# Attention sinks as an extra probability column, and mLSTM memory products placed on strips and row groups, in a two-layer decoder step

## The chip, the core and the metric

The kernel runs on one core of a Trainium2 chip. TensorE (PE) multiplies matrices out of SBUF into PSUM, VectorE (DVE) and ScalarE (ACT) do elementwise work, GpSimd (POOL) and SyncE (SP) issue DMAs. Each engine runs its own instruction stream in order, and streams meet at semaphores. The metric is the device time of one execution in microseconds, the lower the better.

## The reference, cut to what matters

Layer 0 is sliding-window attention with a learned sink per head, layer 1 an mLSTM (a matrix memory). There are 512 prompt tokens and 8 sequences with 4 sample tokens each.

```python
# layer 0, per head: the sink takes part in the maximum and in the sum, not in the output
s = einsum(q, k) * HEAD_DIM ** -0.5 + bias            # 128 queries x 256 keys per block
mx = maximum(max(s), sink)
p = exp(s - mx)
p = p / (sum(p) + exp(sink - mx))
o = p @ v

# layer 1, per head (8 of them), sample tokens: each sequence b has its own memory S[b], 128 x 256
num = a * (qs @ S) + qk @ v
S_new = a_last * S + einsum('s,sd,se->de', wts, k, v)
```

Around them each layer has an input projection, a gate, an output projection and norms over 2048 channels.

## The kernel before

**Weight products.** All large products go through `block`: a weight block of 128 output channels is split into a high and a low part (`w_hi` by ACT in `round_hi`, `w_lo` by DVE in `split_lo`), and for each of 16 tiles of the contraction PE does six matmuls of 272 columns (line 750) into a pair of PSUM banks (`PJ`). A block is called an entry. `PHASES` gives the entries of each phase: `l0` has 8 entries in each of three turns of a loop, `l0z` 10, `l1` 8 for each of 8 heads ("QKVVZOZO").

**Points.** The small work of attention and of the memory is inserted between tiles of the product. In layer 0 every entry has four points, after tiles 4, 8, 11 and 15 (`POINTS`), numbered p = 4e + i (`attend_points`). In the mLSTM every entry has two, after tiles 7 and 15 (`memory_points`): points 0 to 7 of a head lie in its last four entries, point 8 in the first entry of the next head. ACT and DVE have functions `attend(m, p)` and `memory(m, p)` of the same names. In each entry they first empty `PJ` of the entry before, then split the next weights, then do the points; what stands first in this order is done first.

**Attention, per group m (4 of them).** There are 16 softmax steps x; a step is 128 queries of one head in two query blocks, 2 x 256 scores. `scores` makes two steps in one go (line 867), into `MX` banks 0 and 1. `soft` on DVE adds the bias (line 1643), takes the maximum (1645), compares it with the negated sink (1647), and forms the exponent of the sink (1648). ACT does exp of both halves (1242) and of the sink (1244). `norm` on DVE adds the sink's term (1653), takes the reciprocal (1654) and scales (1657). `p_turn` on PE transposes the probabilities (876), ACT copies them out (1235), `pv` multiplies with the values (890), `gate_prompt` on DVE multiplies into the gate (1667). Step x has its `soft` at point 10 + x, its `norm` at 11 + x, its `p_turn` at 12 + x, so at every point from 10 to 28 something is done.

**mLSTM memory, per head.** At point 0 PE transposes k and v (1004, and 1006 for the 32 sample tokens); at 1 it makes k q and spreads three rows of gates over all partitions with weights of 8 rows (1014, 1017); at 2 it makes the chunk updates (1026 to 1031); at 4 the prompt's output (1040 to 1046); at 5 the sample's output; at 7 the update of the eight sample memories `cs` (1065), which DVE adds in (1941); at 8 the norm sums (1072, 1075). Of point 5 the inner part is, for each half of the channels and each of the 8 sequences, one matmul of a 128x128 piece of memory with 4 columns:

```python
mm(MX[:, 3, TS * blk:TS * blk + TS], vs[:, P * blk:P * blk + P], Ds[0:TS, :], start=True, stop=False)   # 1052
for b in range(NB):                                                                                     # 1055
    mm(MX[:, 3, TS * blk + ND * b:TS * blk + ND * b + ND], cs[:, b, P * blk:P * blk + P],
       qa[:, TP + ND * b:TP + ND * b + ND], start=False, stop=(b == NB - 1))
```

An f32 matmul shows as two records in the trace, each with a weight load of its own; an instruction list names it once.

Of the kernel before, what the change touches and what calls it, by code (L numbers as in the profile page):

```python
# [29 lines left out]
P = 128  # L30
# [25 lines left out]
ATT_POINTS = 29  # L56
# [32 lines left out]
C_FIX = 305  # L89
C_NEGD, C_NEGS = 305, 305 + 768  # L90
C_L0 = C_NEGS + 1056
C_CM, C_SM, C_BM = C_L0, C_L0 + 128, C_L0 + 160
C_ALL = C_L0 + 168

def constants():
# [31 lines left out]
    c[0:TS, C_BM:C_BM + NB] = (np.arange(TS)[:, None] // ND == np.arange(NB)[None, :])  # L128
# [7 lines left out]
def offsets(sizes, at=0):  # L136
    out = {}
    for name, size in sizes:
# [10 lines left out]
              ("soft", 1536), ("negd", 768), ("negs", 1056)])  # L149
A1 = offsets([("q", T), ("k", T), ("v", 2 * T), ("vtok", 4 * DV), ("wk", 4 * P), ("rows", 3 * T),  # L150
              ("S", 4 * DV), ("n", 8), ("D", TP), ("qa", T), ("qn", T), ("emt", T), ("h", 2 * T),
              ("cs", NB * DV), ("sb", 3 * TS), ("Ds", TS), ("Uc", 40), ("wc", 40), ("wb", 64),
              ("nsT", 64), ("nout", 72), ("cm", 128), ("sm", 32), ("bm", 8)])
# [36 lines left out]
def trunk(nc, x_prompt, x_sample, c_prompt, c_sample, cache_k, cache_v, state_C, state_n, state_m,  # L190
# [3 lines left out]
    with ExitStack() as ctx:  # L194
# [53 lines left out]
        PP = [soft[:, 0:512], soft[:, 512:1024]]  # L248
        PT = [soft[:, 1024:1536], misc[:, 0:TP]]
# [6 lines left out]
        rows = area(A1, "rows")  # L256
        wks = rows[0:TS, 0:1024].rearrange("p (b e) -> p b e", b=NB)
        ksv = rows[0:TS, 1024:1408]
        ks, vs = ksv[:, 0:P], ksv[:, P:3 * P]
        wbh = rows[0:TS, 1408:1416]  # L260
        GP = slice(64, 64 + MH)
        BP = slice(96, 96 + MH)
        R = rows[GP, :].rearrange("p (j t) -> p j t", j=3)
        RB = rows[BP, :].rearrange("p (j t) -> p j t", j=3)
# [10 lines left out]
        wb = area(A1, "wb").rearrange("p (h b) -> p h b", h=MH)  # L275
        nsT = area(A1, "nsT").rearrange("p (b h) -> p b h", b=NB)
# [62 lines left out]
        om_done, zg_done = sem("om_done"), sem("zg_done")  # L339

# [11 lines left out]
        hout_done, hsq_done = sem("hout_done"), sem("hsq_done")  # L352
        cu_ready, cnew_done, ss1_ready = sem("cu_ready"), sem("cnew_done"), sem("ss1_ready")
# [209 lines left out]
        def _(pool):  # L563
# [92 lines left out]
            pool.dma_start(bm, const[:, C_BM:C_BM + 8]).then_inc(gl_in, 16)  # L656
# [7 lines left out]
            pool.dma_start(nm_p.rearrange("o b h -> h (o b)"), R[:, 2, TP - 1:TP], **SLOW).then_inc(Sp_out, 16)  # L664
            pool.dma_start(nm_s[0].rearrange("b h -> h b"), R[:, 2, TP:T].rearrange("p (b t) -> p b t", t=ND)[:, :, 3], **SLOW)\
# [40 lines left out]
        def _(pe):  # L706
# [164 lines left out]
            def p_turn(m, x):  # L871
# [3 lines left out]
                for c in range(4):  # L875
                    last = tr(MX[:, 2, P * c:P * c + P], PP[x % 2][:, P * c:P * c + P], ident)  # L876
# [19 lines left out]
            def attend(m, p):  # L896
# [1137 lines left out]
```

## Time and profile before

| | |
|---|---|
| median of 3 runs | 2447.22 us (2441.83 to 2449.89) |
| the profiled execution | 2441.93 us, its span 2440.3 us |
| granted TensorE clock over the span | 0.952 |
| PE busy | 2282.1 us, 94% of the span |
| weight product, line 750 | 13152 matmuls in three groups, 293 to 300 ns each |
| one turn of the layer 0 loop | 141.8 us |
| DMA | 300.68 MB, 123 GB/s in the mean |

Durations of matmuls overlap with their neighbours, so a stretch is measured from the start of one row to the start of the next. The number in brackets behind a row of a timeline is the time that its engine stood idle before it, and who ended that. A granted clock of 1.00 is full speed, 0.50 half.

### The profile page before, as it was taken

Reading aid. Unit: us, or ns where it says so; the run is one execution under the profiler, and the core shown is the slowest. Engines: PE = TensorE matmul, PEld = TensorE weight load, DVE = VectorE, ACT = ScalarE, POOL = GpSimd, SP = SyncE. Lnnn points to the kernel's source line nnn. Section 1 sums busy time; section 2 is a strip of 40 time slices with the busy share of each in tenths; the row PEclk is TensorE's granted clock in tenths of the full one; section 3 lists DMA queues with packets and bytes.
Section 4 is the critical chain, followed back from the end, with each engine's and each line's share of the span. In section 5 each row is a group of like instructions: output and inputs, shape, how many; then the busy total and the mean of one; then the engine's idle time right before and its main releaser. Section 6 shows DMA issues by size and latency. Waiting matters only on the chain.

```text
span 2440.3 us, 41297 instructions
## 1 busy us (share of the span) xinstructions
PE 2282.1 (94%) x17089; PEld 2075.9 (85%) x17089; DVE 989.2 (41%) x1561; ACT 682.1 (28%) x1113; POOL 65.2 (3%) x108
## 2 busy tenths in 40 slices
PE   5879999999989999987999999999999999989996
PEld 2469888898988977776999998999999889988995
DVE  1152555737456412137533424343434334352225
ACT  1232343424334322124312212221212121222222
POOL 1000000000000000000000000000000000000000
PEclk8889999999999999988999998999999899989998
DMA  8953213122211599942428346534255345419622
GB/s 319 388 192 87 79 53 90 53 74 69 73 53 53 161 300 297 295 143 98 106 65 100 61 100 75 104 63 107 70 98 70 83 76 96 80 52 294 210 70 74
DMA packets 345755, 300.68 MB, mean 123 GB/s; under 512 B 8561, under 2 KB 287337, under 8 KB 344473
## 3 DMA queue, kind: packets, MB, share of 16 engines
q1 hardware_dynamic: 335952, 247.87, 40.8%
q0 software_dynamic: 9360, 50.19, 5.8%
q8 instruction: 134, 2.20, 0.4%
q10 hardware_dynamic: 290, 0.27, 0.0%
q14 instruction: 19, 0.16, 0.0%
HBM read 274.81 MB, written 27.56 MB: 124 GB/s over the span
## 4 chain that ended last, share of the span: by engine, by line
PE 77%; DVE 8%; DMA 7%; issue 4%; ACT 2%; DVEq 1%; ACTq 0%; SPq 0%
PE PJ L750 59%; DMA obuf<-in_w_ada 3%; DMA raw<-in_w_in_mlstm 3%; PE MX L938 3%; PE MX L1055 1%; ACT w_hi L1148 1%; PE MX L1065 1%; PE MX L876 1%; PE MX L1017 1%; PE MX L867 1%; DVE arena L1643 1%; DVE st L1645 1%; PE MX L890 1%; DMA raw<-in_w_in_attn 1%; DVE w_lo L1497 1%
## 5 line engine op out<-in xcount | busy, mean ns | idle before, releaser
L750 PE MATMUL PJ<-h_hi,w_hi 128*128 128x272 f32 x4384 | 955.1, 300 | 50.9 <-DVE h_lo L1555 23.8
L750 PE MATMUL PJ<-h_hi,w_lo 128*128 128x272 f32 x4384 | 925.0, 293 | 0.0
L750 PE MATMUL PJ<-h_lo,w_hi 128*128 128x272 f32 x4384 | 923.8, 293 | 0.1
L750 PEld LDWEIGHTS PJ<-h_hi,w_hi 128*128 128x128 f32 x4384 | 707.7, 194 | 128.2 <-issue 106.1
L750 PEld LDWEIGHTS PJ<-h_lo,w_hi 128*128 128x128 f32 x4384 | 708.9, 194 | 0.3 <-issue 0.3
L750 PEld LDWEIGHTS PJ<-h_hi,w_lo 128*128 128x128 f32 x4384 | 704.1, 194 | 0.0
L1497 DVE TENSOR_TENSOR w_lo<-raw,w_hi 128x2048 fp32r<-128x2048 f32 x106 | 242.9, 2292 | 431.5 <-ACT w_hi L1148 431.5
L1148 ACT ACTIVATE w_hi<-raw 128x2048 fp32r<-128x2048 f32 x106 | 202.0, 1906 | 42.9 <-DMA raw<-in_w_in_mlstm 33.1
L1242 ACT ACTIVATE arena<-arena,st 128x256 f32<-128x256 f32 x128 | 64.1, 501 | 145.4 <-DVE st L1648 145.4
L1423 ACT ACTIVATE arena<-PJ 128x544 f32<-128x544 f32 x32 | 20.0, 625 | 247.1 <-PE PJ L750 247.1
L1771 DVE COPY modT<-MX 128x36 f32 x16 | 3.1, 196 | 210.6 <-PE MX L949 210.6
L1749 DVE TENSOR_TENSOR w_lo<-raw,w_hi 128x2048 fp32r<-128x2048 f32 x30 | 68.7, 2291 | 36.3 <-ACT w_hi L1324 36.3
L1643 DVE SCALAR_TENSOR_TENSOR arena<-arena,fix,MX 128x512 f32<-128x512 f32 x64 | 47.7, 745 | 68.3 <-PE MX L867 36.6
L1756 DVE TENSOR_TENSOR arena<-arena 128x544 f32<-128x544 f32 x32 | 23.2, 725 | 118.6 <-ACT arena L1315 116.4
L1315 ACT ACTIVATE arena<-PJ 128x544 f32<-128x544 f32 x32 | 20.0, 625 | 177.2 <-PE PJ L750 170.6
L938 PE MATMUL MX<-arena,cT 128*32 128x512 f32 x512 | 68.2, 605 | 0.0
L716 PE MATMUL PJ<-obuf,cT 128*32 128x512 f32 x256 | 42.3, 754 | 26.7 <-DMA obuf<-in_w_ada 26.6
L876 PE MATMUL MX<-fix,arena 128*128 128x128 f32 x256 | 42.1, 288 | 24.4 <-DVE arena L1657 24.4
L1337 ACT ACTIVATE misc<-MX 105x512 f32<-105x512 f32 x16 | 9.6, 598 | 195.2 <-PE MX L938 195.2
L876 PEld LDWEIGHTS MX<-fix,arena 128*128 128x128 f32 x256 | 27.3, 141 | 40.2 <-issue 27.6
L1972 DVE SCALAR_TENSOR_TENSOR obuf<-misc,obuf 128x544 f32 (+1 forms) x16 | 11.6, 725 | 122.7 <-ACT misc L1415 122.7
L1324 ACT ACTIVATE w_hi<-raw 128x2048 fp32r<-128x2048 f32 x30 | 57.5, 1918 | 0.0
(301 smaller groups left out, 1907.2 us busy)
## 6 DMA issues: line engine op xcount, KB each, us to landing
arena<-in_w_ada SPq DMA_DIRECT2D x64, 1024.0 KB, 5.2
raw<-in_w_in_mlstm SPq DMA_DIRECT2D x64, 1024.0 KB, 14.7
raw<-in_w_in_attn SPq DMA_DIRECT2D x40, 1024.0 KB, 5.7
obuf<-in_w_ada SPq DMA_DIRECT2D x32, 1024.0 KB, 10.0
raw<-in_w_out_attn SPq DMA_DIRECT2D x16, 1024.0 KB, 7.9
raw<-in_w_out_mlstm SPq DMA_DIRECT2D x16, 1024.0 KB, 5.9
x_spill<-arena POOLq DMA_DIRECT2D x2, 4352.0 KB, 12.5
arena<-x_spill POOLq DMA_DIRECT2D x2, 4352.0 KB, 14.0
```

Source lines behind the costliest of these rows:

```text
L716: last = mm(PJ[32 * j:32 * j + 32, 2 * pair, :], c_cols(4 * q + j), obuf[:, 4 * (u % 4) + j, 0:512], start=(q == 0), stop=(q == 3))
L750: last = mm(PJ[:, 2 * pair + f, 0:HT], w, h[:, k, HT * f:HT * f + HT], start=(k == 0 and n == 0), stop=(k == KT - 1 and n == 2))
L867: last = mm(MX[:, half, 256 * bl:256 * bl + 256], q0[hs, j, P * b:P * b + P], kk[hs, P * b:P * b + 2 * P], start=True, stop=True)
L876: last = tr(MX[:, 2, P * c:P * c + P], PP[x % 2][:, P * c:P * c + P], ident)
L890: last = mm(MX[64 * half:64 * half + 64, 3, P * bl:P * bl + P], vtok[:, P * (b - 1 + kb) + 64 * a:P * (b - 1 + kb) + 64 * a + 64], PT[half ...
L938: last = mm(MX[32 * i:32 * i + 32, 2, :], c_cols(4 * j + i), u_raw[j][:, 512 * i:512 * i + 512], start=(j == 0), stop=(j == STRIPS - 1))
L1148: fn(w_hi[s][:, :], raw[s][:, :], ACT.Copy).then_inc(hi_done, 1)
L1242: fn(pb, pb, ACT.Exp, bias=st[:, o + 2 + bl:o + 3 + bl], accum_out=st[:, o + 6 + bl:o + 7 + bl]).then_inc(pexp_ready, 1)
L1324: fn(w_hi[s][:, :], raw[s][:, :], ACT.Copy).then_inc(hi_done, 1)
L1497: tt(w_lo[s][:, :], raw[s][:, :], w_hi[s][:, :].bitcast(F32), ALU.subtract)\
L1643: chain(stt(pb, negd[:, 256 * bp:256 * bp + 512], fix[:, ds(head + C_SLP, 1)], MX[:, half, :], ALU.mult, ALU.add))
L1749: tt(w_lo[s][:, :], raw[s][:, :], w_hi[s][:, :].bitcast(F32), ALU.subtract).then_inc(lo_done, 1)
```

## The change

**Attention.** The probability rows get a 257th column for each of the two query blocks, so `PP` is 2 x 257 wide. ACT writes the sink there before the softmax. The maximum and the exp with its running sum then run over 257 columns and take in the sink; lines 1647, 1648, 1244 and 1653 go. A pair of steps is handled at each even point: `p_turn`, `scores`, `p_turn` on PE, two `soft` and two `norm` on DVE, copies and exps on ACT. `pv` and `gate_prompt` go to the odd points. There are 28 points instead of 29.

**mLSTM.** The three gate rows `R` lie on partitions 0, 32 and 64, so the three matmuls of point 1 use three row groups of PE and three banks. Sample k and v are written four times, once to each strip of 32 partitions (point 0, 12 matmuls instead of 3 transposes). At point 5 the queries are the weights, 32 columns, in four column strips, and the memories move, 256 columns; each strip gets the product of all 32 queries with one sequence's memory. ACT copies this out, and a new point 6 picks the right rows with a constant (`C_SS`) and adds them to the rest. At point 7 the eight updates use four row groups and four banks.

```diff
@@ PE attend @@
-                if 14 <= p < ATT_POINTS and p % 2 == 0:
-                    pv(m, (p - 14) // 2)
+                if p >= 12 and p % 2 == 0:
+                    p_turn(m, p - 12)
                 if 10 <= p < 26 and p % 2 == 0:
                     scores(m, (p - 10) // 2)
-                if 0 <= p - 12 < 16:
-                    p_turn(m, p - 12)
+                if p >= 12 and p % 2 == 0:
+                    p_turn(m, p - 11)
+                if p >= 13 and p % 2:
+                    pv(m, (p - 13) // 2)
@@ ACT attend @@
-                    fn(st[:, o + 8:o + 10], st[:, o + 4:o + 6], ACT.Exp).then_inc(pexp_ready, 1)
+                        if x + 2 < 16:
+                            head = g * 8 + (2 * ((x + 2) // 4) + x % 2)
+                            fn(PP[x % 2][:, :, 2 * P:PB], nsink[:, ds(head, 1)].unsqueeze(1).broadcast_to([P, 2, 1]),
+                               ACT.Copy, scale=-1.0).then_inc(sink_set, 1)
@@ DVE soft and norm @@
-                chain(tt(st[:, o + 2:o + 4], st[:, o:o + 2], nsk, ALU.min))
-                tt(st[:, o + 4:o + 6], st[:, o + 2:o + 4], nsk, ALU.subtract).then_inc(pmax_ready, 1)
+                dve.wait_ge(sink_set, val(0, 16, m, x + 1))
+                dve.tensor_reduce(st[:, o:o + 2], pb, AX, ALU.max, negate=True).then_inc(pmax_ready, 1)
-                chain(tt(st[:, o + 10:o + 12], st[:, o + 6:o + 8], st[:, o + 8:o + 10], ALU.add))
@@ PE memory, points 0, 1, 5 and 6, 7 @@
-                        last = tr(MX[0:TS, 3, P * j:P * j + P], src[:, TP:T], ident)
+                        for i in range(4):
+                            last = mm(MX[32 * i:32 * i + 32, 3, P * j:P * j + P], src[:, TP:T], ident,
+                                      start=True, stop=True)
-                        last = mm(MX[:, 1 + j, :], fix[BP, C_ONE:C_ONE + P], RB[:, j, 0:TP],
+                        last = mm(MX[:, 1 + j, :], fix[32 * j:32 * j + MH, C_ONE:C_ONE + P], RB[j],
                                   start=True, stop=True)
+                    pe.wait_ge(abs_done, val(0, 1, m, 1))
+                    for b in range(NB):
+                        j, c = b % 4, b // 4
+                        last = mm(MX[32 * j:32 * j + 32, 2, DV * c:DV * c + DV], qa[:, TP:T], cs[:, b, :],
+                                  start=True, stop=True)
+                    last.then_inc(qc_ready, 1)
+                if p == 6:
+                    pe.wait_ge(qg_done, val(0, 1, m, 1))
                     for blk in range(2):
-                        mm(MX[:, 3, TS * blk:TS * blk + TS], vs[:, P * blk:P * blk + P], Ds[0:TS, :],
-                           start=True, stop=False)
-                        for b in range(NB):
-                            mm(MX[:, 3, TS * blk + ND * b:TS * blk + ND * b + ND],
-                               cs[:, b, P * blk:P * blk + P], qa[:, TP + ND * b:TP + ND * b + ND],
-                               start=False, stop=(b == NB - 1))
+                        o = MX[:, 3, TS * blk:TS * blk + TS]
+                        mm(o, vs[0:TS, P * blk:P * blk + P], Ds[0:TS, :], start=True, stop=False)
+                        for c in range(2):
+                            mm(o, Dm[:, DV * c + P * blk:DV * c + P * blk + P], fix[:, C_SS + TS * c:C_SS + TS * c + TS],
+                               start=False, stop=(c == 1))
-                        last = mm(MX[:, b // 2, DV * (b % 2):DV * (b % 2) + DV], wks[:, b, :], vs,
-                                  start=True, stop=True)
+                        j, c = b % 4, b // 4
+                        rows = slice(32 * j, 32 * j + TS)
+                        last = mm(MX[:, j, DV * c:DV * c + DV], wks[rows, c, :], vs[rows, :], start=True, stop=True)
@@ ACT memory, point 5 (the abs of the sample's sums and the squares go to point 6) @@
+                    act.wait_ge(qc_ready, val(0, 1, m, 1))
+                    act.wait_ge(hp_done, val(0, 1, m, 1))
+                    fn(Dm, MX[:, 2, :], ACT.Copy).then_inc(qg_done, 1)
@@ DVE memory, point 0 @@
-                    ts(rows[BP, :], rows[GP, :], fix[GP, ds(h + (C_ID + 64), 1)], None, ALU.mult).then_inc(rb_done, 1)
+                    ts(RBt[0:GP.stop, :], Rt[0:GP.stop, 0:TP], fix[0:GP.stop, ds(h + C_OH, 1)], None, ALU.mult).then_inc(rb_done, 1)
+                    tt(RS[0:GP.stop], Rt[0:GP.stop, TP:T].unsqueeze(1).broadcast_to([GP.stop, 3, TS]),
+                       O3[0:GP.stop, :, ds(h, 1)].broadcast_to([GP.stop, 3, TS]), ALU.mult).then_inc(rb_done, 1)
-                    tt(wks, MX[0:TS, 3, 0:P].unsqueeze(1).broadcast_to([TS, NB, P]),
+                    tt(wks, MX[:, 3, 0:P].unsqueeze(1).broadcast_to([P, 2, P]),
```

**In what order it stands.** DVE in an attention group, one softmax step and the next, before. Line 1643 is the bias, 1645 the maximum, 1653 to 1657 the normalisation; rows on registers are what the loop needs.

```order
L1643 SCALAR_TENSOR_TENSOR arena<-arena,fix,MX 128x512
L180 REGISTER_ALU
L1645 TENSOR_REDUCE st<-arena 128x2
L180 REGISTER_ALU
L1647 TENSOR_TENSOR st<-st,nsink 128x2
L180 REGISTER_ALU
L1648 TENSOR_TENSOR st<-st,nsink 128x2
L1652 REGISTER_ALU
L1653 TENSOR_TENSOR st<-st 128x2
```

The same place after; 1684 is the bias, 1688 the maximum, 1693 and 1696 the normalisation.

```order
L1684 SCALAR_TENSOR_TENSOR arena<-arena,fix,MX 128x2x256
L191 REGISTER_ALU
L1687 REGISTER_ALU
L1688 TENSOR_REDUCE st<-arena 128x2
L1684 SCALAR_TENSOR_TENSOR arena<-arena,fix,MX 128x2x256
L191 REGISTER_ALU
L1687 REGISTER_ALU
L1688 TENSOR_REDUCE st<-arena 128x2
L1692 REGISTER_ALU
L1693 RECIPROCAL st<-st 128x2
L191 REGISTER_ALU
L1696 TENSOR_SCALAR arena<-arena,st 128x256 x2
```

Two steps now stand in front of the first normalisation, and three of the small operations are gone.

PE at point 5 of an mLSTM head, before, between the weight product (750).

```order
L750 MATMUL PJ<-h_hi,w_lo 128x272 x2
L1052 MATMUL MX<-arena 128x32
L1055 MATMUL MX<-arena 128x4 x8
L1052 MATMUL MX<-arena 128x32
L1055 MATMUL MX<-arena 128x4 x8
L1058 MATMUL MX<-arena,fix 128x32
L1059 MATMUL MX<-arena,fix 128x32
L750 MATMUL PJ<-h_hi,w_hi 128x272 x2
```

After, point 5 (the product is line 765):

```order
L765 MATMUL PJ<-h_hi,w_lo 128x272 x2
L1075 MATMUL MX<-arena 32x256 x8
L765 MATMUL PJ<-h_hi,w_hi 128x272 x2
```

and half a block later point 6, where nothing stood:

```order
L765 MATMUL PJ<-h_hi,w_lo 128x272 x2
L1083 MATMUL MX<-arena 128x32
L1085 MATMUL MX<-fix,arena 128x32 x2
L1083 MATMUL MX<-arena 128x32
L1085 MATMUL MX<-fix,arena 128x32 x2
L1087 MATMUL MX<-arena,fix 128x32
L1088 MATMUL MX<-arena,fix 128x32
L765 MATMUL PJ<-h_hi,w_hi 128x272 x2
```

Sixteen matmuls of four columns became eight of 256 at one point and four of 32 at the next.

## Rows read from the trace of the kernel before

**Rows 1.** The page: engine busy times, and the chain's shares.

```profile
PE 2282.1 (94%) x17089; PEld 2075.9 (85%) x17089; DVE 989.2 (41%) x1561; ACT 682.1 (28%) x1113; POOL 65.2 (3%) x108
...
PE 77%; DVE 8%; DMA 7%; issue 4%; ACT 2%; DVEq 1%; ACTq 0%; SPq 0%
```

**Rows 2.** The page's groups: count | busy, mean ns | idle before, ended by.

```profile
L876 PE MATMUL MX<-fix,arena 128*128 128x128 f32 x256 | 42.1, 288 | 24.4 <-DVE arena L1657 24.4
```

**Rows 3.** Timeline of PE, attention: start, duration, line, form, count, idle before.

```profile
415.02 1.13 PE L867 MATMUL MX<-arena 64*128 64x256 f32 x8
416.08 0.65 PE L876 MATMUL MX<-fix,arena 128*128 128x128 f32 x4
...
421.15 0.65 PE L876 MATMUL MX<-fix,arena 128*128 128x128 f32 x4 [1.41 <-DVE arena L1657]
...
706.18 1.11 PE L876 MATMUL MX<-fix,arena 128*128 128x128 f32 x4 [4.08 <-DVE arena L1657]
```

**Rows 4.** Timelines of DVE and of ACT, one softmax step.

```profile
421.85 0.75 DVE L1643 SCALAR_TENSOR_TENSOR arena<-arena,fix,MX 128x512 f32<-128x512 f32 x1 [0.82 <-PE MX L876]
...
423.35 0.16 DVE L1647 TENSOR_TENSOR st<-st,nsink 128x2 f32<-128x2 f32 x1
...
424.04 0.61 DVE L1657 TENSOR_SCALAR arena<-arena,st 128x256 f32<-128x256 f32 x2
...
423.74 0.51 ACT L1242 ACTIVATE arena<-arena,st 128x256 f32<-128x256 f32 x1 [1.30 <-DVE st L1648]
...
424.74 0.19 ACT L1244 ACTIVATE st<-st 128x2 f32<-128x2 f32 x1
```

**Rows 5.** Timeline of PE, points 0 and 1 of head 1.

```profile
1330.85 0.49 PE L1006 MATMUL MX<-fix,arena 128*32 128x128 f32 x3
1331.10 0.49 PE L750 MATMUL PJ<-h_hi,w_hi 128*128 128x272 f32 x2
...
1338.17 2.84 PE L1017 MATMUL MX<-arena,fix 8*128 8x512 f32 x6
```

**Rows 6.** Timeline of PE, points 5 and 7 of head 2.

```profile
1508.23 0.41 PE L750 MATMUL PJ<-h_hi,w_lo 128*128 128x272 f32 x2
1508.57 0.40 PE L1052 MATMUL MX<-arena 32*128 32x32 f32 x2
1508.90 1.95 PE L1055 MATMUL MX<-arena 128*128 128x4 f32 x16
...
1513.57 0.50 PE L750 MATMUL PJ<-h_hi,w_hi 128*128 128x272 f32 x2
...
1527.30 3.72 PE L1065 MATMUL MX<-arena 32*128 32x256 f32 x16
```

**Rows 7.** Stretches: us, busy and counts, PEclk, DMA share, GB/s; sums of eight and seven.

```profile
342.28:483.99 141.71, 135.71 (x1140) 124.75 (x1139) 80.85 (x181) 57.13 (x137) 4.12 (x6) 1.00 0.25 69
...
706.95:711.31 4.36, 4.36 (x21) 4.11 (x19) 2.61 (x8) 1.78 (x6) 0.00 (x0) 0.50 0.15 37
...
1485.71:1497.83 12.12, 12.12 (x97) 12.12 (x97) 7.25 (x18) 3.12 (x5) 0.56 (x1) 1.00 0.61 52
...
1378.56:1393.30 14.74, 14.74 (x97) 14.60 (x97) 0.77 (x3) 1.40 (x3) 0.00 (x0) 0.81 0.27 60
...
sum 113.88, PE 113.88 PEld 112.71 DVE 6.15 ACT 11.21 POOL 0.00; mean PE 14.23 PEld 14.09 DVE 0.77 ACT 1.40 POOL 0.00
...
sum 55.24, PE 55.24 PEld 54.21 DVE 29.52 ACT 0.32 POOL 6.67; mean PE 7.89 PEld 7.74 DVE 4.22 ACT 0.05 POOL 0.95
...
1852.63:1861.45 8.82, 8.82 (x50) 8.82 (x50) 4.11 (x4) 2.37 (x6) 0.00 (x0) 0.66 0.60 107
```

**Rows 8.** Timeline of PE: 64-column strips in attention, 32-column strips in out0.

```profile
384.08 1.15 PE L848 MATMUL MX<-arena 128*64 128x64 f32 x16
...
857.05 1.07 PE L938 MATMUL MX<-arena,cT 128*32 128x512 f32 x8
```

**Rows 9.** Waits of ACT in the mLSTM: total, times, longest.

```profile
ACT w_hi L1148 <- DMA raw<-in_w_in_mlstm: 33.1, 8, 7.2
```

More of the change, by code:

```diff
@@ L127, in constants @@
     c[0:TS, C_SM:C_SM + TS] = np.where((s // ND == t // ND) & (s <= t), 0.0, BIG)
-    c[0:TS, C_BM:C_BM + NB] = (np.arange(TS)[:, None] // ND == np.arange(NB)[None, :])
+    for j in range(4):
+        for s in range(TS):
+            b = s // ND
+            if b % 4 == j:
+                c[32 * j + s, C_BM + b] = 1.0
+                c[32 * j + s, C_BM + NB + b // 4] = 1.0
+                c[32 * j + s, C_SS + TS * (b // 4) + s] = 1.0
+    for j in range(3):
+        for h in range(MH):
+            c[32 * j + h, C_OH + h] = 1.0
+            c[32 * j + h, C_O3 + MH * j + h] = 1.0
     return c
@@ L247, in trunk @@
         SPs = soft[:, 0:1056]
-        PP = [soft[:, 0:512], soft[:, 512:1024]]
-        PT = [soft[:, 1024:1536], misc[:, 0:TP]]
+        PB = 2 * P + 1
+        PP = [soft[:, 2 * PB * i:2 * PB * i + 2 * PB].rearrange("p (b k) -> p b k", b=2) for i in range(2)]
+        PT = [soft[:, 1028:1540], misc[:, 0:TP]]
         negd, negs = area(A0, "negd"), area(A0, "negs")
@@ L255, in trunk @@
         wk = area(A1, "wk").rearrange("p (c e) -> p c e", c=4)
[L256 to L258 removed]
+        wks = area(A1, "wks").rearrange("p (c e) -> p c e", c=2)
+        ksv, wbh = area(A1, "ksv"), area(A1, "wbh")
         ks, vs = ksv[:, 0:P], ksv[:, P:3 * P]
[L260 removed]
         GP = slice(64, 64 + MH)
[L262 to L264 removed]
+        Rt, RBt = area(A1, "R"), area(A1, "RB")
+        R = [Rt[32 * j:32 * j + MH, :] for j in range(3)]
+        RB = [RBt[32 * j:32 * j + MH, :] for j in range(3)]
+        RS = area(A1, "RS").rearrange("p (j t) -> p j t", j=3)
+        O3 = fix[:, C_O3:C_O3 + 3 * MH].rearrange("p (j h) -> p j h", j=3)
         S = area(A1, "S").rearrange("p (c e) -> p c e", c=4)
@@ L990, in gate_turn @@
                     tr(MX[0:n, 0, 8 * c:8 * c + 8], Ub[:, P * c:P * c + n], ident[GP, 64:72])
-                    tr(MX[0:n, 1, 8 * c:8 * c + 8], Wr[:, P * c:P * c + n], ident[GP, 64:72])
+                    if c < 4:
+                        tr(MX[:, 1, 8 * c:8 * c + 8], Wr[:, P * c:P * c + n], ident[GP, 64:72])
+                for j in range(4):
+                    mm(MX[32 * j:32 * j + 32, 1, 32:40], Wr[:, TP:T], ident[GP, 64:72], start=True, stop=True)
                 pe.wait_ge(gl_in, 96)
@@ L1366, in gate_exps @@
                 act.wait_ge(gate_v, 2)
[L1367 removed]
+                fn(R[1], R[1], ACT.Exp).then_inc(gate_a, 1)
                 fn(Wr, Wr, ACT.Exp).then_inc(gate_a, 1)
@@ L1846, in gate_maxima @@
                 U4 = Ub[:, TP:T].rearrange("p (b t) -> p b t", t=ND)
+                chain(dve.memset(Rt[0:GP.stop, :], 0.0))
                 chain(dve.memset(tg[:, 0:1], 0.0))
@@ L1864, in gate_maxima @@
                          M4[:, :, 3:4].broadcast_to([MH, NB, ND]), ALU.subtract))
-                chain(ts(R[:, 0, :], Mr, -1.0, None, ALU.mult))
-                tt(R[:, 2, :], Bc, Mr, ALU.add).then_inc(gate_v, 1)
+                chain(ts(R[0], Mr, -1.0, None, ALU.mult))
+                tt(R[2], Bc, Mr, ALU.add).then_inc(gate_v, 1)
                 dve.wait_ge(gate_v, 2)
```

120 lines of the change are left out of this document (65 added, 55 removed).

## The prediction

> **What bounds the kernel now.** I read the engine totals first: TensorE (PE) is busy 94% of the span, VectorE (DVE) 41%, and 77% of the chain that ended last is PE [rows 1]. So a microsecond counts where PE waits, where PE does work that could be shorter, or where its clock is low. The change touches all three. Second, PE's own waits: in all attention groups it waits 24.4 us before the transposes of line 876, for DVE's normalisation in line 1657 [rows 2]. Third, the timeline of PE inside an attention group and inside an mLSTM head, from start to start of its rows, because durations of pipelined matmuls overlap. Fourth, stretches of the weight product right behind the mLSTM points, with the clock that they were granted.
>
> **Part 1, the attention softmax.** Before, PE transposes one step's probabilities at every point, and the points lie at tiles 4, 8, 11 and 15 of a block. A pair of score matmuls ends at 416.1, the transpose that needs its softmax step is due four tiles of product later, and PE stands 1.41 us before it [rows 3]. In the last group, where DVE also gates Z blocks, one wait is 4.08 us [rows 3], and the 4.36 us behind it ran at half clock [rows 7], which cost another 2.2 us. After, a pair of steps is handled at even points only, so seven or nine tiles of product lie between scores and the next transposes instead of three or four. Seven tiles take 5.3 us (six matmuls a tile, 96 in 12.12 us [rows 7]), the product at the odd point about 1 us, the first transpose 0.4: PE comes back 6.7 us after its scores.
>
> Is the pair ready? From the rows: multiply-add with reduction ends 1.5 us after it starts, exp of both halves takes 1.0, the two scalings 0.6 and with the small reciprocal ahead of them 0.8 [rows 4]. DVE does two softmax steps back to back (3.0 us), ACT the exps behind each, so the first step is normalised about 3.8 us and the second about 5.0 us after the scores. Against 6.7 us that leaves 2.9 us. DVE's weight splitting (2.3 us) can push the pair at tile 4 back by about 1 us; that is covered. DVE loses three small operations a step (0.16 us each) and ACT swaps one small exp (0.19) for one small copy [rows 4]; neither bounds anything there, so I cost them at nothing. DVE was busy 80.9 us of the 141.7 of a group [rows 7], so if that cover were gone it would still be PE that ends last; the work saved would show as more idle DVE. I take 27 us off: 24.4 and 2.2 and a little for restarts, with new waits between 0 and 17 us as the bound from below, so 10 to 30.
>
> **Part 2, the mLSTM products, work on PE.** Per head, all at full clock:
> - Point 0. Three narrow transposes take 0.25 us [rows 5]. They become twelve matmuls, 24 records of 32 weight columns, in four column strips. Lower bound is the column time, three groups of two records of 0.107, 0.64 us; upper bound the 0.083 us a record of the present three, 2.0 us. The nearest row is 64-column strips with short moving operands, 16 records in 1.15 us, so 0.07 each [rows 8], and narrower weights should not be slower: I take 1.25 us. **+1.0.**
> - Point 1. Three matmuls of 8 rows and 512 columns take 2.8 us one after another [rows 5]. On three row groups and into three banks they may overlap: between 0.9 us (one of the three alone is 0.93) and 2.8. I take 1.1. **-1.7.**
> - Point 5. Sixteen matmuls with 128x128 weights for 4 columns each, and six small ones, take 5.0 us [rows 6]. After, eight matmuls of 32 weight columns and 256 moving columns. The same strip form with 512 columns takes 1.07 us for four [rows 8], so two rounds of 256 take 1.05. The new point 6 keeps the small ones and adds four of 32 columns at about 0.12 a record: 2.2 us, and one more interruption of the product costs 0.1. **-1.6.** If strips did not overlap, 16 records of 0.23, as at point 7, would make it +1.0.
> - Point 7. Eight matmuls of 32 rows take 3.7 us one after another [rows 6]. Four row groups and four banks could give 0.86. The nearest row has two row groups of 64: eight records of the same 256 columns in 1.06 us, where serial would be 1.7 and perfect overlap 0.86 [rows 3], as if each weight load took about 0.13. Sixteen of these make 2.0 us. **-1.7.**
>
> Together -4.0 us a head, 32 us in eight heads; the bounds give a loss of 22 to a gain of 49.
>
> What each new wait holds up: point 5 now waits for the absolute values of point 4, which ACT makes right behind point 4, half a block earlier. Point 6 waits for ACT's copy, which follows its rounding of the next weights; PE asks half a block, 6 us, after point 5. ACT now stands at point 6 until PE is in mid-block, after it has rounded the next weights, so no load and no split is behind it; DVE likewise. Cost nothing. The one memset and few instructions more in the gate phase are below 1 us.
>
> **Part 3, the clock.** Behind point 5 the product's 96 matmuls should take 12.12 us at granted clock 1.00 [rows 7]; in the eight heads they take 113.88 us together, 16.9 more, at granted clocks like 0.81. Behind point 7, 48 should take 6.06 and take 55.24 in seven heads, 12.8 more [rows 7]. One level is 2.4 GHz and the other 1.2. Before each fall PE had done 5 us of four-column matmuls or 3.7 us of 32-row ones. Behind point 1 (2.8 us of 8-row matmuls) it fell in head 5 with no other wait (8.82 us at 0.66 [rows 7]) and in part in head 0, 4 us for both. The thin points themselves, where the clock had fallen before they ended, and the last head's I put at 5, an estimate from these. In all about 38 us. The stretch of 12.12 us at 1.00 lies behind point 2, which ends in one-column and narrow matmuls too. The new points are 1.05, 2.2, 2.0 and 1.1 us long, all shorter than the shortest that ever set it off. I take 35 of 38 back.
>
> The Trainium skill, "TensorE: Matmul & The Clock Gate", section "Part 1: The HAM clock gate (the "warmup" mystery)", says that the gate is driven by how busy the array has been, and idle or sparse stretches bring half rate; by that rule the drops are from the thin points, and the trace agrees with falls to half rate directly behind them.
>
> **Sum.** 27 + 32 + 35 = 94 us off. The profiled execution took 2441.9 us, the median of the runs is 2447.2. So 2348 against the one and 2353 against the other; I say 2352.
>
> **A rule that speaks against it.** Changing the row or column division of the array shows in the trace as a gap of 0.09 us (0.34 from start to start before line 1052, where a pair of product matmuls takes 0.25 elsewhere) [rows 6]; the new points change it about as often as the old. The Trainium skill, "TensorEngine Tiling (Array Packing)", section "Key Properties", says that switching the tiling mode drains TensorE; by the row it is worth less than 1 us a head either way.
>
> **Rivals.**
> - A, the forecast: 2352, chance 0.58.
> - B, row groups overlap fully at point 7 and point 0 runs at its column time: 2.0 becomes 0.9, 1.25 becomes 0.65; 1.7 us a head, 14 us, so 2338. For it: strips overlap fully in [rows 8]. Against: the 1.06 us of 64-row groups. Chance 0.20. The Trainium skill, "TensorE: Matmul & The Clock Gate", section "Part 3: Packing small matmuls — row/col tiling", gives this rule: a pack of tiles takes one matmul's time and about 4 ns for each further tile. No run before has four row groups.
> - C, the clock still falls, since the thin points come in the same number and only shorter: part 3 is worth 0 to 10 us. 2447 - 59 - 5, so 2383. For it: a fall also followed 2.8 us of thin work in two of eight heads. Chance 0.14.
> - D, small matmuls do not overlap at all (four row groups never appear before, and narrow records are bound by their weight loads): point 0 +1.8, points 5 and 6 +1.0, points 1 and 7 nothing, 22 us more, clock as before; only part 1 remains: 2447 + 22 - 27 = 2442. Chance 0.05, no change.
> - E, slower: the pair is late. PE comes back 6.7 us after its scores and needs the first step at 3.8, so the point from which it decides is a DVE that starts the pair 2.9 us late, behind the splitting of weights. There are 32 even points; each us beyond that costs 32 us, and a wait of 4 us also brings half clock, as seen. To end slower it must be 6.3 us late at each, a wait of 3.4: 2447 - 94 + 32 x 3.4 = 2462. Against: DVE's largest single job there is 2.3 us. Chance 0.03.
>
> **From cases to numbers.** About 0.3% is what a measurement of this kernel can tell from no change, 7 us. A, B and C are faster, with D split between same and slower. Faster 0.93, same 0.03, slower 0.04. The range: A's own, with its bounds (part 1 at 10 to 30, the overlaps of part 2 near the values taken, 18 to 42, part 3 at 28 to 38), is 2337 to 2391; with B and most of C, 2334 to 2394.
>
> **What would show it.** In the profile after: waits for the normalisation before the transposes near 0; point 1 at 1.1 us, point 5 at 1.05, point 6 at 2.2, point 7 at 2.0 and point 0's narrow part at 1.25; granted clock 1.00 in the stretches behind points 5 to 7; each head some 8 us shorter. It would be wrong if row groups run one after another, if half clock stays, or if waits for weights (33.1 us of ACT [rows 9]) grow because heads are shorter: eight of these waits cost PE little now.

## The result, and the profile after

The changed kernel takes 2376.85 us (median of 4 runs, 2369.48 to 2381.01), the kernel before 2447.48 (4 runs). The ratio is 0.9711, 95% interval 0.9682 to 0.9741: 70.6 us faster, where 94 off, 2352, was forecast. The profiled execution took 2381.01 us.

From the page of the changed kernel, engine busy times and the chain's shares, which answer to [rows 1]:

```profile
PE 2210.6 (93%) x17200; PEld 2012.6 (85%) x17200; DVE 947.7 (40%) x1378; ACT 688.3 (29%) x1121; POOL 65.1 (3%) x108
...
PE 80%; DMA 9%; DVE 6%; issue 3%; ACT 2%; DVEq 1%; ACTq 0%; SPq 0%
```

PE is busy 72 us less, and is still the bound. In attention, all waits of PE in the stretch 320 to 800 (total, times, longest), which answer to [rows 2]:

```profile
PE PJ L765 <- DVE h_lo L1617: 3.2, 1, 3.2
PE MX L891 <- ACT arena L1270: 2.8, 4, 0.8
PE PJ L765 <- issue: 2.6, 2, 1.3
```

The waits for DVE's normalisation are gone. Left are 0.7 to 0.8 us a group at the last even point, 2.8 in all: no scores stand between the two transposes of the last pair there, and the second waits until ACT has copied the first out.

In the heads of the mLSTM, timeline of PE (start, duration, count), points 0, 1, 5, 6 and 7, answering to [rows 5, 6]:

```profile
1304.47 0.86 PE L1027 MATMUL MX<-fix,arena 128*32 128x128 f32 x24
...
1312.38 1.13 PE L1039 MATMUL MX<-arena,fix 8*128 8x512 f32 x6
1313.45 0.52 PE L765 MATMUL PJ<-h_hi,w_hi 128*128 128x272 f32 x2
...
1345.43 1.07 PE L1075 MATMUL MX<-arena 128*32 128x256 f32 x16
...
1352.64 0.40 PE L1083 MATMUL MX<-arena 32*128 32x32 f32 x2
...
1361.20 1.15 PE L1096 MATMUL MX<-arena 32*128 32x256 f32 x16
1371.27 0.82 PE L765 MATMUL PJ<-h_hi,w_hi 128*128 128x272 f32 x2 [8.92 <-issue]
```

Point 7 fell from 3.7 to 1.1 us. But the last row is new: behind point 7, where the next head begins, PE stands 8.92 us, and no other engine ends that wait. Waits of PE in the heads (1200 to 2180 us before, 1180 to 2120 after), before:

```profile
PE PJ L750 <- issue: 8.4, 3, 4.6
PE MX L1072 <- DVE arena L1941: 3.3, 1, 3.3
```

and after:

```profile
PE PJ L765 <- issue: 31.2, 7, 8.9
PE PJ L765 <- DVE w_lo L1539: 5.8, 1, 5.8
PE MX L1102 <- DVE arena L1987: 3.6, 1, 3.6
```

Of these 37.0 us before product matmuls, 31.8 lie right behind point 7 in the six turns where the loop goes back (8.9, 2.6, 5.8, 3.0, 8.5, 3.1); before it was 8.6. The 5.8 is one of the six: its split ended when the fetch had come too.

**What the wait is.** PE's sequencer (PEldq) has a record for the loop's own instructions. Line 1122 of the changed kernel and line 1092 of the one before, duration min/median/max in ns:

```profile
L1122 PEldq COMPARE_BRANCH  x7: 83/3812/9685, 1361.3 to 2109.0; - x7
```

```profile
L1092 PEldq COMPARE_BRANCH  x7: 83/3495/7947, 1393.4 to 2168.7; - x7
```

The seventh is the exit and takes 0.08 us. The six that go back take 3.3 to 9.7 us, **in both kernels**. The sequencer runs ahead of the array: before, the first of them starts at 1393.42, when the 3.7 us of point 7 have just been handed over, lasts 6.71 us, and the array stands only 3.38. After, the branch starts at 1361.32, the array has 1.0 us left, and the branch lasts 9.69.

What is fetched can be seen among the DMA queues. The branch of 3.32 us at 1495.76, 40 slices of its time:

```profile
GB/s 0 0 0 0 0 0 0 0 0 0 0 0 193 0 0 0 0 0 0 0 0 0 0 0 0 0 0 0 0 0 0 0 0 0 0 0 0 0 0 0
...
q8 instruction: 1, 0.02, 1.8%
```

One packet of instructions, 1.0 us after the branch began, and nothing else in flight. The first 7.3 us of the branch of 9.69 us, 1361.3 to 1368.6:

```profile
DMA packets 820, 0.42 MB, mean 58 GB/s; under 512 B 13, under 2 KB 818, under 8 KB 820
...
q1 hardware_dynamic: 818, 0.41, 25.3%
q0 software_dynamic: 2, 0.01, 0.3%
```

All but two are packets of a weight load (q1). The instruction packet starts at 1368.64, 7.3 us after the branch, when 818 of the load's last 833 packets have gone. The same pattern is in the traces of all eight kernels of this study whose loops are not written out, 64 branches that go back: 44 met at most 39 weight packets in their first 2 us, their fetch started 0.9 to 1.5 us in, and they took 3.3 to 3.8 us; 20 met 211 or more, the fetch started after 2.2 to 7.3 us, and they took 4.6 to 9.7. That the weight load is what holds the instruction packet back is read from this pattern; no run moved a load away from a branch. The loop over attention groups is one of the long ones: its two branches take 3.3 us each in the changed kernel, no weight load is near them, and the array stands 1.3 us behind each: the matmuls still queued there hide the rest. The short loops of the output products, two blocks a turn, do without a fetch at their branches; no instruction packet starts between 924 and 1056 us, where three of them go back. They take 0.21 to 0.25 us when they go back and 0.07 to 0.08 at the exit:

```profile
L445 PEldq COMPARE_BRANCH  x14: 67/214/248, 820.3 to 2317.0; - x14
```

The Trainium skill, "Advanced Engine Details and Errata", section "Control Flow Timing", gives about 108 ns for a compare-and-branch; the short loops come near it here, the long ones do not. By that rule the short loops fit and the attention loop does not; the trace agrees, with no packet at the short branches and one behind each long one. The head loop is near the limit by its records, but it takes nine packets of 16 KB a turn, one more than eight lines; the trace does not show why a turn that by its records would just fit is fetched anew.

### The profile page after: what moved, and what is told of

Same layout as the page of the kernel before. It is cut to its first block, busy times and chain, and to the rows that moved or that the text cites. A ratio compares the mean times of both kernels' runs of the same rounds, so it can differ in the third digit from the quotient of the medians.

```text
span 2379.4 us, 41279 instructions
## 1 busy us (share of the span) xinstructions
PE 2210.6 (93%) x17200; PEld 2012.6 (85%) x17200; DVE 947.7 (40%) x1378; ACT 688.3 (29%) x1121; POOL 65.1 (3%) x108
## 4 chain that ended last, share of the span: by engine, by line
PE 80%; DMA 9%; DVE 6%; issue 3%; ACT 2%; DVEq 1%; ACTq 0%; SPq 0%
PE PJ L765 63%; DMA raw<-in_w_in_mlstm 5%; DMA obuf<-in_w_ada 3%; PE MX L955 3%; PE MX L882 1%; PE MX L891 1%; PE MX L905 1%; DVE w_lo L1539 1%; DMA raw<-in_w_in_attn 1%; PE PJ L731 1%; ACT w_hi L1178 1%; PE MX L1105 1%; PE MX L863 1%; PE MX L800 1%; DVE obuf L1591 1%
## 5 line engine op out<-in xcount | busy, mean ns | idle before, releaser
L765 PEld LDWEIGHTS PJ<-h_hi,w_hi 128*128 128x128 f32 x4384 | 698.3, 191 | 158.8 <-issue 129.8
L765 PEld LDWEIGHTS PJ<-h_lo,w_hi 128*128 128x128 f32 x4384 | 701.1, 192 | 5.7 <-issue 5.7
L765 PEld LDWEIGHTS PJ<-h_hi,w_lo 128*128 128x128 f32 x4384 | 696.1, 192 | 0.0
L1178 ACT ACTIVATE w_hi<-raw 128x2048 fp32r<-128x2048 f32 x106 | 202.3, 1909 | 40.2 <-DMA raw<-in_w_in_mlstm 32.2
L1281 ACT ACTIVATE arena<-arena,st 128x257 f32<-128x257 f32 x128 | 64.3, 503 | 60.8 <-DVE st L1688 60.8
L731 PEld LDWEIGHTS PJ<-obuf,cT 128*32 128x32 f32 x256 | 6.3, 120 | 49.3 <-DMA obuf<-in_w_ada 27.3
L1688 DVE TENSOR_REDUCE st<-arena 128x2 f32<-128x514 f32 x64 | 44.1, 689 | 6.4
L800 PE MATMUL MX<-arena,fix 128*128 128x272 f32 x128 | 36.9, 446 | 10.3 <-ACT arena L1194 10.0
```

The source lines that it names most:

```text
L731: last = mm(PJ[32 * j:32 * j + 32, 2 * pair, :], c_cols(4 * q + j), obuf[:, 4 * (u % 4) + j, 0:512], start=(q == 0), stop=(q == 3))
L765: last = mm(PJ[:, 2 * pair + f, 0:HT], w, h[:, k, HT * f:HT * f + HT], start=(k == 0 and n == 0), stop=(k == KT - 1 and n == 2))
L800: last = mm(MX[:, f, 0:HT], ones, sqb[:, k % 2, HT * f:HT * f + HT], start=(k == 0), stop=(k == KT - 1))
L1178: fn(w_hi[s][:, :], raw[s][:, :], ACT.Copy).then_inc(hi_done, 1)
L1281: fn(pb, pb, ACT.Exp, bias=st[:, o + bl:o + 1 + bl], accum_out=st[:, o + 6 + bl:o + 7 + bl]).then_inc(pexp_ready, 1)
L1688: dve.tensor_reduce(st[:, o:o + 2], pb, AX, ALU.max, negate=True).then_inc(pmax_ready, 1)
```

## The experiments

All are timed against the kernel before on the same chip. "Half clock" is how much longer than at full clock (12.12 us a block) the product's stretches behind a point took, without PE's waits. It holds a little that is no clock: at granted clock 1.00 a stretch of half a block takes 6.12 to 6.21 us and not 6.06, so up to 0.15 us a stretch is the restart of the product.

### Attention alone, mLSTM alone

Each half of the change as in its diff, the other undone.

> The kernel before with the attention part of the change alone (257th column, pairs of steps at even points), the mLSTM untouched. The prediction's part 1: 24.4 us of waits before the transposes go and 2 to 3 us of half clock, so 27 us off, 2420 (2416 to 2432). Rival: part of the gain comes back in the issue waits of the mLSTM, which lie where the weight loads fall; then only 10 to 15 us off, about 2435.

Measured: 2421.70, 0.9886 (0.986 to 0.9912), 26.9 us off, as expected; the rival's 10 to 15 lies outside the interval, 21 to 34.

> The changed kernel with its attention part undone, the mLSTM part alone. By the prediction 32 us of work and 35 of clock off: 2380. By the theory that the loop's back branch of PE was hidden behind the slow matmuls of point 7 and is now in the open (34 us of issue waits behind point 7 in the changed kernel against 12 before): 2447 less 43, about 2404 (2396 to 2412).

Measured: 2400.84, 0.9805 (0.9783 to 0.9828), 47.8 us off. That is within the range of the theory of the branch, and 21 us short of what the prediction gives. Its trace has the same gaps behind point 7, 30.4 us together. (The 34 and 12 us in the expectation are issue waits of the whole kernels; behind point 7 alone it is 31.8 and 8.6.) The parts add up to 74.7, within their intervals the 70.6 of both. What is missing against the forecast is missing in the mLSTM: 67 forecast, 48 found.

### The loop written out

```diff
-            with pe.Fori(0, MH - 1) as r:
-                layer1((r, 1), (r, 0))
+            for r in range(MH - 1):
+                layer1((None, r + 1), (None, r))
```

> The changed kernel with PE's loop over the mLSTM heads written out, so PE has no back branch there; nothing else differs. Theory branch: the six gaps of 2.6 to 8.9 us behind point 7 (31.8 us together) are the fetch of instructions after the branch; they go, and with them 5 to 12 us of half clock behind them: 2377 less 40, 2337 (2325 to 2348). Rival: PE waits there for the split of the next weights, which DVE does behind the update of the memories, or for DMA; then the gaps stay and the time moves by less than 5 us.

Measured: 2354.66, 0.962 (0.9598 to 0.9642), 22 us faster than the changed kernel, and slower than the expected range. All six gaps behind point 7 are gone, and half clock behind point 7 fell from 9.0 us to 0.4. Seven stretches of half a block behind point 7, their sums, changed kernel and written out (6.06 each at full clock):

```profile
sum 51.38, PE 51.38 PEld 51.38 DVE 14.43 ACT 2.87 POOL 6.31; mean PE 7.34 PEld 7.34 DVE 2.06 ACT 0.41 POOL 0.90
```

```profile
sum 42.84, PE 42.84 PEld 42.84 DVE 40.77 ACT 19.18 POOL 6.31; mean PE 6.12 PEld 6.12 DVE 5.82 ACT 2.74 POOL 0.90
```

So the gaps were the branch and nothing that DVE or the memories' transfers do there. Of the 40 us 22 came, since other waits stand now, each behind a load of weights that was late (PE, heads):

```profile
PE MX L1036 <- DVE arena L1940: 7.8, 2, 5.0
PE PJ L765 <- DVE w_lo L1539: 7.1, 2, 3.7
```

The same edit in the kernel before:

> The kernel before with PE's loop over the heads written out. Theory branch: its branches lie behind the 3.7 us of matmuls of point 7 that are still queued, so only about 9 us of gaps are to be had, and a few of half clock: 2436 (2430 to 2442). If the branches cost what their records last (28.8 us in six) whatever is queued, it would be 2418.

Measured: 2455.78 (10 runs, 2447.91 to 2466.13), 1.0033 (1.0016 to 1.005). The expectation fell: no gain. The gaps behind point 7 went there too, but others came, two pairs of waits for late weights (10.6 us) and one wait of 5.5 us in straight code, with an instruction packet in it. The trace is of the fastest of the ten executions, 2447.91, so it does not show the 8 us between that one and the median. This run leaves open what a branch is worth alone; the next two tell.

### Point 7 slow again, with and without a branch

```diff
-                        rows = slice(32 * j, 32 * j + TS)
+                        rows = slice(0, TS)
```

> The changed kernel with all eight updates of point 7 on row group 0, so one after another (they read the first strip's values, so the new memories of most sequences are other numbers; sizes are the same). Point 7 back at 3.7 us: 2.6 us a head, 21 us more work. Theory branch (the queued matmuls cover the branch): six branches are covered for 2.6 us each again, 16 us back, and the half clock behind the point is 12.8 instead of 9.0: 2377 + 21 - 16 + 4 = 2386 (2380 to 2394). Rival, the wait has nothing to do with point 7's length: 2377 + 21 + 4, and more clock, 2402 to 2410.

Measured: 2377.28, 0.972 (0.9695 to 0.9744), the same as the changed kernel. That is 9 us better than expected: the gaps gave back 18 us where 16 were counted, the waits behind point 8 fell from 7.0 us to 2.4 and the half clock behind it from 2.9 to 0.4 (the four blocks there take 48.30 at full clock). The two profiled executions differ by 4.5 us already where the mLSTM begins, so part of the 9 may be chance. PE's timeline at the first boundary:

```profile
1360.82 3.90 PE L1096 MATMUL MX<-arena 32*128 32x256 f32 x16
1369.26 0.59 PE L765 MATMUL PJ<-h_hi,w_hi 128*128 128x272 f32 x1 [4.54 <-issue]
```

The branch there started at 1360.9 and took 8.06 us. The six branches took 3.5 to 9.3 us, as in the changed kernel, but the gaps are 13.9 us together instead of 31.8: 21 us more work, 18 us less standing.

> The same as p7_one_group (eight updates on row group 0, other numbers in most new memories) with PE's loop over the heads written out, so there is no branch to cover. Theory branch: the full price of point 7 against the written-out changed kernel (2354.7): 21 of work and 8 to 12 of half clock, 2386 (2378 to 2392), about what the looped one takes. If slack at the waits for weights takes up the longer heads: 10 less, 2376.

Measured: 2384.72, 0.9751 (0.9723 to 0.9779). The four corners, as ratios to the kernel before:

| | point 7 in 1.1 us | point 7 in 3.7 us | price of slow |
|---|---|---|---|
| loop | 0.9711 | 0.9720 | 2 us |
| written out | 0.9620 | 0.9751 | 32 us |

Each price has an interval of some 10 us either way. With a branch behind it the fast point 7 is worth nothing that can be told; without one it is worth 32 us. That is a net price: in the traces point 7 itself costs 25 us more when slow and the half clock behind points 6 and 7 another 25, while waits for late weights and the half clock behind them shrink by some 13. That settles where this term went.

### Thin work and the clock

Point 5 in its old form, nothing at point 6; ACT and DVE do at point 5 again what had gone to point 6:

```diff
-                    for b in range(NB):
-                        j, c = b % 4, b // 4
-                        last = mm(MX[32 * j:32 * j + 32, 2, DV * c:DV * c + DV], qa[:, TP:T], cs[:, b, :],
-                                  start=True, stop=True)
+                    for blk in (0, 1):
...
+                        for b in range(NB):
+                            mm(MX[:, 3, TS * blk + ND * b:TS * blk + ND * b + ND],
+                               cs[:, b, P * blk:P * blk + P], qa[:, TP + ND * b:TP + ND * b + ND],
+                               start=False, stop=(b == NB - 1))
```

> The changed kernel with point 5 in its old form: two halves of a small matmul and eight of four columns each, nothing at point 6. Work: 5.0 to 6.2 us against 1.0 + 2.4, 16 us in eight heads. Clock theory: half clock returns behind point 5 (17.0 us against 1.2, less the 4.1 that lie behind point 6 now), 12 us. 2377 + 28 = 2405 (2398 to 2412). Rival, the clock was healed by something else (fewer waits at the head's end): 2393.

Measured: 2397.84, 0.9806 (0.978 to 0.9832), 23 us slower by the ratios, less than the 28 expected. Half clock behind point 5 is 13.7 us, in all eight heads, as the clock theory has it. Points 5 and 6 cost 21.5 us more in the trace (some of that at half clock), where 16 of work were counted. What makes the time smaller is the branch again: two of the six branches met a weight load here, where three did in the changed kernel, and the gaps behind point 7 are 18.9 us instead of 31.8.

The same, in two halves (against the last one):

```diff
                 if p == 5:
-                    for blk in (0, 1):
+                    for blk in (0,):
+                if p == 6:
+                    for blk in (1,):
```

> As p5_thin, but the first half of the thin matmuls (2.0 to 2.4 us) stands at point 5 and the second at point 6, half a block later: the same work in two shorter stretches, 13 us more than the changed kernel. If the length of one thin stretch decides, no half clock follows: 2377 + 14 = 2391 (2386 to 2396). If thin work in sum decides, or 2.4 us is already long enough, the falls stay: 2403 to 2408.

Measured: 2388.36, 0.9757 (0.9732 to 0.9783). The time fits the theory of length, the trace does not; that the time fits is chance, since the gaps behind point 7 are 21.5 us here instead of 31.8. Eight stretches behind the first half (2.14 us of thin work), two of them and the sum; full clock would be 48.5:

```profile
1226.27:1233.99 7.72, 7.72 (x50) 7.57 (x49) 2.29 (x1) 0.39 (x1) 0.00 (x0) 0.78 0.29 58
1346.36:1352.55 6.19, 6.19 (x50) 6.04 (x50) 2.29 (x1) 0.50 (x1) 0.00 (x0) 1.00 0.17 28
...
sum 57.13, PE 57.13 PEld 55.96 DVE 18.34 ACT 3.83 POOL 0.00; mean PE 7.14 PEld 6.99 DVE 2.29 ACT 0.48 POOL 0.00
```

The same work is followed by half clock in five heads and not in three; behind the second half it falls in all eight (63.22 us). Against p5_thin the half clock behind the points is larger (23.5 against 13.7), and only the points themselves, which run less at half clock inside, are shorter (40.9 us in all against 48.5). So splitting thin work does not heal the clock. The changed kernel's 1.00 us at point 5 is never followed by a fall, its 2.37 us at point 6 in two heads of eight, and the same 2.37 us in eight of eight in p7_one_group_unroll. Length makes a fall likely but does not decide it alone; what else does stays open.

Point 1 on one row group:

```diff
-                        last = mm(MX[:, 1 + j, :], fix[32 * j:32 * j + MH, C_ONE:C_ONE + P], RB[j],
+                        last = mm(MX[:, 1 + j, :], fix[0:MH, C_ONE:C_ONE + P], RB[0],
```

> The changed kernel with the three matmuls of point 1 all on row group 0, so one after another (all three spread the first row of gates, so the mLSTM's numbers are others; sizes are the same). Work: 2.8 against 1.06 us in eight heads, 14 us. Clock: behind point 1 the old kernel lost 9.7 us, the changed one 0.8; if the 2.8 us of thin work alone set it off, 5 to 9 us more. 2377 + 14 + 7 = 2398 (2390 to 2402). Rival, the falls behind point 1 came from its waits and not from its length: 2391 or, with branches met at better moments, 2386.

Measured: 2396.2, 0.9775 (0.9747 to 0.9803), 16 us by the ratios. Point 1 costs 1.7 us more a head as expected, 14 us in all, and half clock behind it is back, eight stretches:

```profile
sum 57.51, PE 57.51 PEld 57.51 DVE 31.80 ACT 22.45 POOL 0.00; mean PE 7.19 PEld 7.19 DVE 3.98 ACT 2.81 POOL 0.00
```

9.0 us over the 48.5 at full clock, in four heads, as in the kernel before (9.6). No wait stands ahead of point 1 here, so the falls come from the three matmuls running one after another, not from waits. The same length is followed by no fall in the other four heads, so here too it does not decide alone. That the time shows 16 and not 23 is within what the intervals allow.

### Both loops written out

Beside the loop over the heads, as above, the loop over the attention groups:

```diff
-            with pe.Fori(0, GR - 1) as r:
-                layer0("l0", (r, 0), (r, 0))
+            for r in range(GR - 1):
+                layer0("l0", (None, r), (None, r))
```

> The changed kernel with both of PE's loops written out, that over the attention groups too. There two branches show gaps of 1.3 us each in the trace, behind no thin work, so 2.6 us: 2352 (2349 to 2355), hard to tell from the one with the head loop alone. If straight code costs fetches of its own in attention, where no branch was near a load of weights, it would be slower by 1 to 5.

Measured: 2327.5 (5 runs, 2325.03 to 2329.25), 0.9505 (0.9491 to 0.9518). The best kernel of the study, and 27 us below the one with the head loop alone written out, where 2.6 were expected. The trace puts hardly any of it in attention: the gaps behind the two branches, 3.1 us, are gone, but 2.7 of waits for DVE (line 845) stand there now, and both kernels reach the mLSTM at 1166 us. Behind that PE's waits for late weights are nearly gone:

```profile
PE MX L1048 <- DVE arena L1943: 1.8, 1, 1.8
PE PJ L765 <- issue: 1.6, 2, 1.0
```

PE's waits for late weights fell from 14.9 us to 3.4, and the half clock around them by some 11; that is most of the 28 between the two profiled executions. ACT waited 70.5 us for weights of the heads with one loop written out, longest 16.5, and 31.8 us, longest 6.0, with both. Both programs have the same weight loads. The two slowest with one loop written out took 35.1 and 33.5 us to land and take 16.5 and 15.1 with both, where another one is slowest, 31.3. Why is open.

The head loop alone written out, with small transfers of the memories:

```diff
-                pool.dma_start(C_out[ds(at, 1)].rearrange("o k b e -> (o k) b e"), cs).then_inc(cs_out, 16)
+                pool.dma_start(C_out[ds(at, 1)].rearrange("o k b e -> (o k) b e")[:, 0:1, :], cs[:, 0:1, :]).then_inc(cs_out, 16)
...
-                    pool.dma_start(cs, C_in[ds(h + 1, 1)].rearrange("o k b e -> (o k) b e")).then_inc(cs_in, 16)
+                    pool.dma_start(cs[:, 0:1, :], C_in[ds(h + 1, 1)].rearrange("o k b e -> (o k) b e")[:, 0:1, :]).then_inc(cs_in, 16)
```

> The changed kernel with PE's head loop written out, and store and load of the eight sample memories cut to one of the eight each (the other seven are not written out or loaded, so those numbers are others). In the written-out kernel two pairs of waits are left, 14.9 us, each behind a load of weights that took 30 us while the memories were stored and loaded. If the two transfers disturb each other, the waits go and the half clock behind them: 2354.7 - 15 - 6 = 2334. If the weights are slow by themselves, no change, 2350 to 2356.

Measured: 2344.53 (2332.6 to 2350.57), 0.9583 (0.9565 to 0.9601), between the two expectations. In its trace 7.5 us of the 14.9 of waits are left, and two loads still take 31 and 29 us; but the trace is of the fastest execution, 12 us below the median. So the transfers of the memories may have a share in it, and late weights come without their full size. The kernel with both loops written out has the full transfers and hardly a wait, so they alone do not bring the waits about. What does stays open.

The kernel before with both loops written out:

> The kernel before with both of PE's loops written out; beside the changed kernel with both written out (2327.5) it shows what the change is worth where PE has no branch. Theory branch: all that the change takes off then counts, 27 in attention, 47 of work in the heads and some 25 of half clock, about 99: 2327.5 + 99 = 2427 (2420 to 2434), 21 below the kernel before. Rival: written-out code meets slow loads of weights, as the kernel before with the head loop alone written out did (2455.8); then 2445 to 2460, and the change is worth 120 or more there for a reason that is not the branch.

Measured: 2426.76 (5 runs, 2426.15 to 2430.28), 0.9933 (0.9919 to 0.9948), as expected. There the heads lose no time behind point 7 either. Between the two kernels with both loops written out the change is worth 99 us by the medians and, since the kernel before was 5 us slower beside the one than beside the other, 105 by the ratios (0.9505 / 0.9933 = 0.957).

## Why the prediction was right, and where it was off

2376.85 lies in the range 2334 to 2394, but 25 us above the value. Step by step:

- **Part 1, 27 us.** Right. All waits for the normalisation went, 2.8 us of new ones came (0 to 17 were allowed for), att_only gave 26.9, and E (the pair late) did not happen; DVE had the slack that was counted.
- **Part 2, 32 us.** The overlaps hold, and two terms, points 0 and 7, were taken too long. From start to start, at full clock: point 0's strips 0.79 us instead of 1.25 (0.033 a record); point 1 1.06, against 1.1; point 5 1.00, against 1.05; point 6 2.37, against 2.2; point 7 1.1 instead of 2.0. Points 2 and 8 became 0.3 shorter together, which was not counted. That is 5.6 us a head, 45 in all, so rival B's conditions all but held (1.1 and 0.79, where it has 0.9 and 0.65); but its 2338 is farther off than the forecast, because of the missing term below. The Trainium skill, "TensorE: Matmul & The Clock Gate", section "Part 3: Packing small matmuls — row/col tiling", gives one matmul's time and about 4 ns for each further tile of a pack. The trace agrees nearly: the two rounds of four at point 7 take 1.08 us where perfect overlap of the 3.72 would be 0.93.
- **Part 3, 35 us.** Half right. Half clock behind point 1 fell from 9.6 to 0.8 us and behind point 5 from 17.0 to 1.2, and the granted clock behind both is 1.00 in all heads, but 4.1 stands behind point 6, in two heads at 0.78 (the sums of eight stretches behind points 5 and 6, of 48.5 at full clock, below). Behind point 7 it fell only from 12.8 to 9.0: the thin work that set it off was replaced by an idle gap that does the same. Written out, it is 0.4. Behind point 8 it rose from 0 to 2.9. Behind all five together it fell from 39.4 to 18.0, and the 8.6 that lay inside points 1 and 5 went: about 30 came back. There was also more to be had than the 38 of the working: 48, since behind point 1 only heads 0 and 5 were counted, 4 us, while heads 2 and 6 fell too, and the inside of the points was put at 5.
```profile
sum 49.71, PE 49.71 PEld 48.54 DVE 23.88 ACT 16.89 POOL 0.00; mean PE 6.21 PEld 6.07 DVE 2.98 ACT 2.11 POOL 0.00
...
sum 52.58, PE 52.58 PEld 51.41 DVE 6.16 ACT 11.22 POOL 0.00; mean PE 6.57 PEld 6.43 DVE 0.77 ACT 1.40 POOL 0.00
```

- **The missing term.** This is the step that failed: point 7 was costed at PE's work and the clock behind it alone. Its matmuls were also the cover of the loop's back branch, 3.3 us or more in each of six turns, and the working asked only what hid an edit's new costs, not what the shortened work itself had hidden. 31.8 us of gaps against 8.6 is 23 us; about 5 more are fetches and waits behind point 8. 27 + 45 + 30 - 28 = 74, and 70.6 were measured (63 to 78 by the interval). So the forecast is off by less than its mistakes: part 2 gave 13 more than was counted, part 3 gave 5 less, and the term at nothing took 28.
- **Waits for weights**, which I named as what would make it wrong, did not grow (ACT 32.2 us against 33.1). They come when the gaps go, as after_unroll shows.

The chance of 0.93 for faster was well placed. The forecast 2352 is in effect one for kernels without the branch: there the change is worth 99 to 105 us, where 94 were forecast. In those two traces half clock gives back 36 us, as counted, and the work 45 instead of 32.

## What to carry to other kernels

When work ahead of a loop's end gets shorter, look at the sequencer's record of the branch, not only at the engine's gaps: a long body fetches its first instructions at every turn, and the queued work that hides this costs next to nothing, so shortening it gains next to nothing. Such a loop can be written out, but measure it: in the changed kernel that gave 22 us for one loop and 49 for both, in the kernel before nothing for one (1.0033; late weights came in place of the gaps) and 0.7% for both. To keep a body as short as the two-block loops here, or bulk loads away from the moment of the branch, follows from the traces and was not tried. Small matmuls on four row groups, or four column strips, do overlap almost fully, and wide moving operands in place of 4-column ones also spare the clock behind them.

## What the runs showed of the hardware that was not expected

- A back branch of a long loop takes PE's sequencer 3.3 us or more, and up to 9.7 us where a load of weights is in flight and its instruction packet starts late. How long the array stands depends on what is queued: in the changed kernel 1.3 us behind the branches of attention, 2.6 to 8.9 behind those of the heads. From the start of the instruction packet to the end of the branch it is 2.3 to 2.9 us in 60 of the 64, and 4.0 to 4.1 in four.
- Straight code can wait for instructions too: 4.31 us in the changed kernel at 1382.95, 14 product matmuls after point 8, with an instruction packet at 1384.84 and PE going on 2.4 us later.
- Loads of the same 1 MB of mLSTM weights land in 9.4 to 27.3 us in the changed kernel, and up to 35.1 in the one with the head loop written out. In all eight kernels with PE's head loop kept, the slowest takes 26.3 to 27.3 us; in all six with it written out, 30.5 to 35.3. Which loads are slow differs between programs that differ only in PE's loops, and with the waits and half clock that follow it is most of the 27 us between two of them. The cause is open.
